# The down projection of three FFNs by seven products: a two-layer hybrid decoder step on one core

## The reference

```python
def swiglu_half(x, g, w_up, w_down):
    h = rmsnorm(x, g)
    gate, up = jnp.split(h @ w_up, 2, axis=-1)
    return x + 0.5 * ((jax.nn.silu(gate) * up) @ w_down)
```

## Time and profile before

| | us |
|---|---|
| median of 3 runs | 2964.17 |
| lowest and highest | 2961.67, 2966.86 |
| the profiled execution | 2963.34 |
| its span in the profile | 2961.5 |

### The profile page before, as it was taken

One profiled execution on the slowest core, in us unless ns is written; L12 is line 12 of the kernel. 1 busy time (PEld: TensorE's weight loads), 2 busy tenths in 40 slices (PEclk: granted clock), 3 DMA queues, 4 the chain that ended last, 5 costly groups with the idle time before them and its releaser, 6 DMA issues.

```text
span 2961.5 us, 59957 instructions
## 1 busy us (share of the span) xinstructions
PE 2904.4 (98%) x23276; PEld 2823.8 (95%) x23276; DVE 1607.9 (54%) x2331; ACT 926.6 (31%) x1555; POOL 1604.1 (54%) x1466
## 2 busy tenths in 40 slices
PE   8999999999999999999999999999999999999998
PEld 8999999989989899999999999999999989999998
DVE  7463775534432567373784737745343334783745
ACT  4121233032132325252452524321302423351423
POOL 6676676545553575425455244765555545744343
PEclk9999999999999999999999999999999999999999
DMA  5786859745521344353444433797364223443532
GB/s 196 191 258 193 213 170 283 181 160 150 137 86 58 111 141 139 128 170 111 128 142 132 160 115 106 234 243 208 117 163 124 78 69 103 156 149 120 171 118 84
DMA packets 196941, 444.05 MB, mean 150 GB/s; under 512 B 13464, under 2 KB 57664, under 8 KB 195904
## 3 DMA queue, kind: packets, MB, share of 16 engines
q1 hardware_dynamic: 106944, 280.08, 29.2%
q0 software_dynamic: 40128, 125.83, 17.7%
q10 hardware_dynamic: 49664, 35.30, 3.9%
HBM read 422.64 MB, written 144.35 MB: 191 GB/s over the span
## 4 chain that ended last, share of the span: by engine, by line
PE 88%; DVE 7%; PEld 1%; ACT 1%; DMA 1%; issue 1%; POOL 0%; ACTq 0%; DVEq 0%; POOLq 0%
PE dense L681 53%; PE SA L741 14%; PE SB L741 11%; PEld dense L681 1%; PE SA L881 1%; PE SA L968 1%; PE SA L867 1%; DMA raw<-wst 1%; PE SA L952 1%; PE SA L808 1%; DVE tmp L1479 1%; DVE Hl L1484 1%; PE SB L964 1%; PE SA L955 1%; PE SA L852 0%
## 5 line engine op out<-in xcount | busy, mean ns | idle before, releaser
L551 POOL TENSOR_SCALAR Wh<-raw 128x512 fp32r<-128x512 f32 x620 | 458.0, 739 | 787.6 <-PEq L686 509.3
L553 POOL TENSOR_TENSOR Wl<-raw,Wh 128x512 fp32r<-128x512 f32 x620 | 853.4, 1376 | 51.7
L681 PE MATMUL dense<-Hh,Wh 128*128 128x272 f32 x2784 | 592.2, 294 | 22.5 <-DVE Hl L1470 10.5
L681 PE MATMUL dense<-Hh,Wl 128*128 128x272 f32 x2784 | 577.9, 289 | 0.0
L681 PE MATMUL dense<-Hl,Wh 128*128 128x272 f32 x2784 | 576.8, 289 | 0.0
L681 PEld LDWEIGHTS dense<-Hh,Wh 128*128 128x128 f32 x2784 | 438.8, 189 | 36.3 <-issue 21.9
L681 PEld LDWEIGHTS dense<-Hl,Wh 128*128 128x128 f32 x2784 | 439.9, 190 | 0.0
L681 PEld LDWEIGHTS dense<-Hh,Wl 128*128 128x128 f32 x2784 | 437.4, 190 | 0.0
L616 POOL TENSOR_TENSOR Sl<-pair,Sh 128x512 fp32r<-128x512 f32 x120 | 171.4, 1447 | 411.6 <-ACT Sh L1048 410.8
L681 PE MATMUL dense<-Ah,Wh 128*128 128x272 f32 x1408 | 292.6, 289 | 0.1
L681 PE MATMUL dense<-Al,Wh 128*128 128x272 f32 x1408 | 290.5, 287 | 0.0
(11 more groups left out here) (459 smaller groups left out, 6294.6 us busy)
## 6 DMA issues: line engine op xcount, KB each, us to landing
raw<-wst SPq DMA_DIRECT2D x276, 512.0 KB, 3.6
w_sums<-wst POOLq DMA_DIRECT2D x36, 1536.0 KB, 13.9
w_sums<-wst POOLq DMA_DIRECT2D x18, 2048.0 KB, 16.5
pair<-wst SPq DMA_DIRECT2D x120, 256.0 KB, 3.5
pair<-w_sums SPq DMA_DIRECT2D x60, 512.0 KB, 3.7
wsum<-w_sums SPq DMA_DIRECT2D x60, 512.0 KB, 3.6
w_sums<-w_sums POOLq DMA_DIRECT2D x12, 1536.0 KB, 12.3
wsum<-wst SPq DMA_DIRECT2D x60, 256.0 KB, 2.6
```

What stands on the lines that cost most here:

```text
L551: pool.tensor_scalar(Wh[:, j, cs], raw[:, j, cs], 1.0, 0.0, ALU.mult, ALU.add).then_inc(glink, 1)
L553: pool.tensor_tensor(Wl[:, j, cs], raw[:, j, cs], f32(Wh[:, j, cs]), ALU.subtract).then_inc(glink, 1)
L681: mm = pe.matmul(dps[slot][:, a, 0:HALF], w[:, ring, w0:w0 + 128], x[:, k, a * HALF:(a + 1) * HALF], start=(k == 0 and n == 0), stop=(k == ...
```

## The change

In the FFNs `f` = 1, 2, 3 the first 16 inner tiles go through the down projection by seven products too. The weights of two output tiles, eight inner tiles deep, are again 2 by 2 groups of four blocks, so four steps do what eight dense tiles did. The last six inner tiles stay dense.

For that, each pair of inner tiles (tile t and t + 4 of a block) is also needed in four mixtures of token halves. GpSimd makes them in the step after the pair is complete (`mixed_sums`, four operations of 272 columns), ScalarE makes their high part (`mixed_hi`, 1088 columns in one), GpSimd the low part (`mixed_lo_part`, 1088 columns in one). The inner tiles are therefore done in the order `HIDDEN`, and kept in high and low parts in `PH`, `PL`, `QH`, `QL`; two of the four sets lie where `raw`, `Wh` and `Wl` are, which are not used then. The first step of a down block waits before its second product for the mixtures' low parts (`mix_lo`).

An inner tile's split is moved from the end of its step to the step after (`hidden_behind`), and the step order is written out (`STEPS`): 7 up, 4 down, 8 up, 4 down, 5 up. One up step lies between a block's last inner tile and its down steps. The low part of A22 goes from VectorE to GpSimd. On GpSimd the order inside a step is: sums of a pair, lows of S2 and S1, low of the mixtures, low of A22. The sums of the down weights need 16 more transfers for each of the three FFNs: issued at mixer pieces 54 to 84 for `f` = 1 and 3, and one per step in `f` = 1 for `f` = 2. The 24 others move from pieces 1 to 45 to pieces 6 to 52. The pieces of the dense last block are loaded and split during the last three steps.

```diff
+HIDDEN = [b * FF_BLOCK + p // 2 + p % 2 * (FF_BLOCK // 2) for b in range(2) for p in range(FF_BLOCK)]
+HIDDEN += range(2 * FF_BLOCK, FF_TILES)
...
+STEPS = [("up", i) for i in range(FAST_AT[1] + 1)] + [("down", o) for o in range(DOWN_PAIRS)]
+STEPS += [("up", i) for i in range(FAST_AT[1] + 1, FAST_AT[2] + 1)]
+STEPS += [("down", DOWN_PAIRS + o) for o in range(DOWN_PAIRS)]
+STEPS += [("up", i) for i in range(FAST_AT[2] + 1, FAST)]
+LAST_DOWN = [s for s, x in enumerate(STEPS) if x[0] == "down" and x[1] % DOWN_PAIRS == DOWN_PAIRS - 1]
+LATE = (FAST_AT[1], FAST_AT[2])
+assert len(STEPS) == PAIRS
+SUM_AT = (1, FF_BLOCK, 2 * FF_BLOCK, FF_TILES)
...
-BY_DVE, BY_POOL = (A11, A12, S3, S4, A22), (S2, S1)
+BY_DVE, BY_POOL = (A11, A12, S3, S4), (S2, S1, A22)
...
 PIECE_BASE = [EXTRA + l * STREAM for l in range(DEPTH)]
 SUM_STEPS, THREE_STEPS = 6, 2
-SUMS_AT = (*range(1, 28, 3), *range(3, 28, 3), 38, 39, 41, 42, 44, 45)
+SUMS_AT = tuple(range(6, 54, 2))
+DOWN_SUMS_AT = tuple(range(54, 86, 2))
...
-                done = ONE + LOW0[f] + (i - 1) * DVE_LO
+                if what == "down" and i % DOWN_PAIRS == 0:
+                    c = i // DOWN_PAIRS
+                    sp.wait_ge(sum_down[c], 16 * SUM_STEPS * f)
+                    sp.sem_inc(pair_began, 1)
+                    sp.wait_ge(sum_down3, 16 * THREE_STEPS * (2 * (f - 1) + c + 1))
...
-                sp.wait_ge(q_lo_pool, ONE + POOL0[f] + i * POOL_LO)
+                sp.wait_ge(q_lo_pool, ONE + POOL0[f] + (s * POOL_LO - 1 if s else 0))
                 sp.dma_start(pair[:, S2:S1 + 1, :], w_sums[0:2, n, :, :].rearrange("s p c -> p s c")).then_inc(s21_in, 16)
                 low_made(A12)
                 sp.dma_start(slot(A12), wst[at, :, 512:1024]).then_inc(a12_in, 16)
                 low_made(S4)
                 sp.dma_start(wsum[:, 0:2, :], w_sums[2:4, n, :, :].rearrange("s p c -> p s c")).then_inc(s34_in, 16)
-                low_made(A22)
+                sp.wait_ge(q_lo_pool, ONE + POOL0[f] + s * POOL_LO)
...
+                def last_down(m):
+                    load(p0 + DOWN_AT[0][2] + m, d0 + 6 * FF_BLOCK + 2 * FF_LAST + m, m % 2, FF_LAST * P)
+                for s in range(1, PAIRS):
+                    load_seven(f, s)
+                    if s == PAIRS - 3:
+                        sp.wait_ge(prod_done, 7 + (PAIR0[f] + LAST_DOWN[1] + 1) * 7)
+                        sp.sem_inc(pair_began, 1)
+                        last_down(0)
+                        last_down(1)
...
+            def down_sums(f, at):
+                if at < 12:
+                    sum_step(f, 3 + at % 2, at // 2)
+                else:
+                    three_step(f, 3 + (at - 12) // 2, at % 2)
+            def mixed_sums(f, which, hp):
+                if hp:
+                    pool.wait_ge(pair_mid, (UP0[f] + 2 * hp - 1) * 3 + 3)
+                else:
+                    pool.wait_ge(slot_free[1], ONE + TILE_BASE[f // 2] // 2 + ((0, FFN2_T0)[which] // 2 + 2))
+                pool.sem_inc(split_began, 1)
+                n = HID_PAIRS * (f - 1) + hp
+                if n:
+                    pool.wait_ge(mix_lo, n)
+                    pool.sem_inc(split_began, 1)
+                h0, h1 = slice(0, HALF), slice(HALF, TOK)
+                E, O, T = tmp[:, 0, :], tmp[:, 1, :], mixed[which]
+                pool.tensor_tensor(T[:, 0, :], E[:, h0], E[:, h1], ALU.subtract).then_inc(mix_sum, 1)
+                pool.tensor_tensor(T[:, 1, :], E[:, h1], O[:, h1], ALU.subtract).then_inc(mix_sum, 1)
+                pool.wait_ge(mix_sum, 4 * n + 1)
+                pool.tensor_tensor(T[:, 3, :], T[:, 0, :], O[:, h1], ALU.add).then_inc(mix_sum, 1)
+                pool.wait_ge(mix_sum, 4 * n + 3)
+                pool.tensor_tensor(T[:, 2, :], T[:, 3, :], O[:, h0], ALU.subtract).then_inc(mix_sum, 1)
+            def mixed_lo_part(f, which, hp):
+                pool.wait_ge(mix_hi, HID_PAIRS * (f - 1) + hp + 1)
+                pool.tensor_tensor(mixed_lo(which, hp % 4), mixed[which], f32(QH[hp % 4][:, :, :]),
+                                   ALU.subtract).then_inc(mix_lo, 1)
...
-                    for m in range(1, KT):
-                        one(p0 + DOWN_AT[0][b] + m, nf * P)
+                for s, (what, i) in enumerate(STEPS):
+                    mixes = what == "up" and i % 2 == 0 and i <= LATE[1]
+                    if mixes:
+                        mixed_sums(f, which, i // 2)
+                    if s + 1 < PAIRS:
+                        lows(f, s + 1, (S2, S1))
+                    if mixes:
+                        mixed_lo_part(f, which, i // 2)
+                    if s + 1 < PAIRS:
+                        lows(f, s + 1, (A22,))
+                    if f == 1 and s < 16:
+                        down_sums(2, s)
+                    if s >= PAIRS - 3:
+                        one(p0 + DOWN_AT[0][2] + s - (PAIRS - 3), FF_LAST * P)
+                for m in range(3, KT):
...
+                def fast(i, part, sums_made=None):
...
+                                pe.wait_ge(mix_lo, sums_made)
                         if copied:
                             pe.wait_ge(prod_copy, n * 2 + copied)
                         if read:
                             pe.wait_ge(prod_read, n * 5 + read)
...
+                    elif b == 0:
+                        for s, (what, i) in enumerate(STEPS):
+                            if what == "up":
+                                fast(s, normed)
+                                continue
+                            c = i // DOWN_PAIRS
+                            if i % DOWN_PAIRS == 0:
+                                pe.wait_ge(ffn_lo, f * FF_TILES + FF_BLOCK * (c + 1))
+                                pe.sem_inc(step_began, 1)
+                            fast(s, hidden_part, HID_PAIRS * (f - 1) + (c + 1) * HID_PAIRS // 2)
+                    if b < 2 and not alternate:
...
+                def hidden_hi(h):
+                    j = h % 2
+                    if h >= 2 * FF_BLOCK:
+                        ins = act.activation(Ah[:, h - 2 * FF_BLOCK, :], tmp[:, j, :], ACT.Copy)
+                    elif j == 0:
+                        ins = act.activation(PH[h % FF_BLOCK // 2][:, 0, :], tmp[:, 0, 0:HALF], ACT.Copy)
+                    else:
+                        ins = act.activation(PH[h % FF_BLOCK // 2][:, 1:3, :], halves(tmp[:, 1, :]), ACT.Copy)
+                    ins.then_inc(ffn_hi, 1)
...
+                def mixed_hi(hp):
+                    act.wait_ge(mix_sum, 4 * (HID_PAIRS * (f - 1) + hp) + 4)
+                    act.activation(QH[hp % 4][:, :, :], mixed[which], ACT.Copy).then_inc(mix_hi, 1)
+                def up_products(s, i):
...
+                    ahead(s, A11, S2)
+                    hidden_behind(s)
                     act.wait_ge(ffn_lo, t - 1)
+                    if i < 2 * FF_BLOCK:
+                        act.wait_ge(mix_sum, 4 * (HID_PAIRS * (f - 1) + i // 2) + (2, 4)[j])
+                    if i - 1 in LATE:
+                        act.wait_ge(down_x, 3 * 2 * DOWN_PAIRS * (f - 1) + 3 * DOWN_PAIRS * (LATE.index(i - 1) + 1))
                     act.wait_ge(prod_done, 7 + n * 7 + 3)
                     act.activation(tmp[:, j, HALF:TOK], SB[:, 0, 0:HALF], ACT.Copy).then_inc(prod_copy, 1)
-                    if ahead:
-                        for q in (S1, A12, S3, S4):
-                            high(f, a + i + 1, q)
+                    ahead(s, S1, A12)
+                    if j == 0 and i <= LATE[1]:
+                        mixed_hi(i // 2)
+                    ahead(s, S3, S4)
                     act.wait_ge(prod_read, n * 5 + 7)
-                    act.wait_ge(pair_mid, n * 3 + 2)
+                    act.wait_ge(pair_mid, u * 3 + 2)
                     act.activation(tmp[:, 4 + j, :], tmp[:, 4 + j, :], ACT.Silu).then_inc(silu_done, 1)
-                    if ahead:
-                        high(f, a + i + 1, A22)
-                    act.wait_ge(pair_mid, n * 3 + 3)
-                    act.activation(Ah[:, hidden_at(i, a, b), :], tmp[:, j:j + 1, :], ACT.Copy).then_inc(ffn_hi, 1)
+                    ahead(s, A22)
...
+                def down_products(s, d):
+                    n, e = PAIR0[f] + s, 2 * DOWN_PAIRS * (f - 1) + d
+                    act.wait_ge(prod_read, n * 5 + 3)
+                    act.wait_ge(prod_done, 7 + n * 7 + 1)
+                    act.activation(tmp[:, 3, 0:HALF], SA[:, 0, 0:HALF], ACT.Copy).then_inc(prod_copy, 1)
+                    ahead(s, A11, S2)
+                    if e:
+                        act.wait_ge(down_x, 3 * e - 2)
+                    act.wait_ge(prod_done, 7 + n * 7 + 3)
+                    act.activation(tmp[:, 5, HALF:TOK], SB[:, 0, 0:HALF], ACT.Copy).then_inc(prod_copy, 1)
+                    ahead(s, S1, A12, S3, S4, A22)
...
+                def up_products(s, i):
+                    n, u = PAIR0[f] + s, UP0[f] + i
+                    t = L * (2 * FF_TILES) + (which * FF_TILES + 2) + i
```

(51 more changed lines are left out.)

276 lines of the change are left out of this document (176 added, 100 removed).

## The result

The changed kernel takes 3004.3 us (median of 4 runs, 3000.5 to 3016.7) against 2965.2: ratio 1.0147, interval 1.0133 to 1.0161. It is slower by 1.5%; the forecast was 2948, with a range of 2926 to 2970, and "slower" had a chance of 0.15. The profiled execution took 3000.45 us.

What follows compares the result with a forecast made beforehand. TensorE, busy 98% of the span, was taken to bound the kernel. 2963.3 - 36.2 (matmuls removed) + 17.4 (stalls in six blocks) + 3 (transfers in the first FFN) = 2947.5; beside the median 2948 us, range 2926 to 2970.

Steps and rivals of the forecast that it cites:

- The 288 matmuls: Six down blocks: 48 fewer TensorE matmuls each, at 0.1256 us, all on the path; 36.2 us saved.
- ScalarE's copy: Up steps: one more ScalarE copy of 1088 columns per two steps, 1.3 us taken, no cost by itself.
- GpSimd's long subtraction: Even up steps: one GpSimd subtraction of 1088 columns per pair, 2.55 us taken, bounds 2.5 to 3.8.
- turns by whole instructions: VectorE and GpSimd at the port: each holds the other for its own instruction's time less about 0.14 us.
- the second product of the first down step: Entry of a down block: TensorE waits 1.35 us for the last pair's long subtraction; 8.1 us over six.
- the list: Expected TensorE waits: first down step's second product (1 to 2 us, six times); first read or copy in odd steps.
- the walk: Up steps followed instruction by instruction with port turns: 1.55 us for three pairs, 2.9 a block, 17.4 for six.
- The odd step works most of the lag off: Odd up step after a pair: lag mostly recovered, next pair's sums 0.6 late, costing 0.65 us.
- the lag adds up: Rival in up steps: later pairs start 2 us late, 7.7 us per block, 2977 us; chance 0.28 including partly so.
- The ledger: Port time in two up steps: 20.5 us of VectorE and GpSimd turns in 21.1, so the order decides.
- The first of the FFNs: First of the three FFNs: GpSimd's 16 added transfer issues delay the sums; 3 us taken, between 0 and 7.
- The mixers: Moved and added sum transfers in the mixers: zero taken, plus and minus 3 us.

Runs made afterwards that it cites:

- e6: The changed kernel with the low part of A22 back on VectorE, last in its step; 2990.4 us.
- e1: The changed kernel with VectorE's read of the sixth product queued ahead of its low part of S3 in an up step; 3001.1 us.
- e7: The changed kernel with a mixer's 24 old sums back at pieces 1 to 45, the 16 new ones unmoved; 3000.0 us.
- e8: The changed kernel with the 16 transfers of f = 1 issued in the first mixer instead, at pieces 55 to 85; 3031.6 us.
- e10: The changed kernel with TensorE's wait for mix_lo at the second product's fourth inner tile, and sum transfers moved and spread; 3004.2 us.
- e5: The changed kernel with GpSimd's long subtraction one step later, in the odd step, for pairs not last in a block; 3006.2 us.
- e2: The changed kernel with the long subtraction of 1088 columns split into four of 272; 3000.7 us.
- e4: The changed kernel with both edits of e1 and e2: read ahead of S3's low, long subtraction in four pieces; 3005.0 us.
- e3: The changed kernel with the long subtraction on VectorE, between its low of S4 and the gate, not on GpSimd; 2986.7 us.
- e9: The changed kernel with the long subtraction on VectorE in the odd step, except a block's last pair, kept in its own step; 2990.1 us.
- e12: The changed kernel with long subtraction (one step later) and low of A22 on VectorE, TensorE's mix_lo wait at the fourth inner tile; 2976.6 us.
- e13: e12 with a block's last long subtraction ahead of product 6, sums at pieces 1 to 45 and 48 to 78, three-steps every fourth; 2964.7 us.
- e16: e13 with all sums issued at the changed kernel's pieces; 2970.6 us.
- e11: The changed kernel with a pair's sums and long subtraction on VectorE, and TensorE's mix_lo wait at the fourth inner tile; 2977.8 us.
- e15: e13 with the sums of a pair on VectorE too, GpSimd keeping the lows of S2 and S1; 2960.2 us.
- e17: e15 with a pair's sums ahead of the low of A11 and of the inner tile's low part; 2960.0 us.

## Why the prediction was wrong

**What held.** The 288 matmuls at 0.1256 us; a step still 10.55 us where nothing waits; ScalarE's copy (1.1 us, 1.3 taken); GpSimd's long subtraction (2.67 to 2.99 us, 2.55 taken from the earlier trace rows); turns by whole instructions (a low of VectorE 3.02 us behind one of 2.75); the PSUM reads never stretched (0.42 to 0.44, all 300 in the up steps). And most of the places: TensorE stopped at the second product of the first down step, at the first read and at the copy in odd steps, as listed. The largest wait, for VectorE's read of product 6, was not on the list.

**The step that failed** is this one of the walk: "The odd step works most of the lag off; the next pair starts its sums 0.6 late and costs 0.65." The first pair of a block came out nearly as walked. In the step shown above (begun at 2633.46) the long subtraction ran from 9.1 to 11.9 us instead of 10.5 to 12.9, the gate product ended at 13.2 as in the walk, and TensorE lost 0.5 us, not 0.25 (0.8 in the other block of that FFN). But the odd step behind it worked nothing off. GpSimd's lows lay across it too. Last of all its low of A22, which the change had moved from VectorE, held VectorE's last value, and the next pair's sums wait for that value (that step began at 2655.03):

```profile
2657.72 1.31 POOL L715 TENSOR_TENSOR Sl<-wsum,Sh 128x512 fp32r<-128x512 f32 x1 [4.93 <-ACT Sh L1190]
2659.89 1.31 POOL L699 TENSOR_TENSOR mixedM<-tmp 128x272 f32<-128x272 f32 x1 [0.86 <-DVE tmp L1857]
```
```profile
2658.26 1.35 DVE L1857 TENSOR_TENSOR tmp<-tmp 128x544 f32<-128x544 f32 x1
```

The sums began 4.9 us into their step, 2.1 later than the 2.8 of the walk and not 0.6; in all twelve such pairs of the last two FFNs it is 4.7 to 5.2. Their long subtraction then ended some 14.6 us after the start of their step, with the gate product behind it, and such a pair cost 3.2 us, not 0.65. The first down step cost 2.65 (1.9 of it the wait for the long subtraction), not 1.35. e6 supports this reading: with the low of A22 back on VectorE two steps take 23.1 us, 1.2 less.

That is the condition of the rival "the lag adds up": "If the second and third pair of a block start 2 us late, not 0.6". It was the right mechanism, had 0.28, and was itself too cheap: 2 us a pair and 7.7 a block, where a pair cost 3.2 and 66 us over six blocks are 11 a block.

A second thing in the walk was wrong: whose turn it is. The walk served VectorE's low of S3 ahead of the long subtraction. In the trace GpSimd's next instruction follows its last at once, and the low comes behind it, with the read of product 6 and the gate product behind that low. In e1 the read goes ahead; in the same pair the long one ended at 2671.16 and the gate product at 2672.07, and TensorE waited 1.46 for the copy. The four kernels that change the order alone give 0.3 to 0.9 us of the 3.2 of a pair, so this is the smaller part.

**The ledger.** The prediction said: "20.5 us of turns in 21.1. It fits only just, so the order decides." The two steps took 24.3. The sum that the later forecasts used adds all of VectorE's work in two up steps (14.7 us) to GpSimd's at the port (13.4): 28.1 us. It counts eight reads of PSUM (0.43 each) where there are ten, so every sum in this table should be 0.9 higher; the differences stay. In the last FFN, which has no transfers of sums in it, and in TensorE's starts in the last two FFNs:

| kernel | sum, us | two steps, us | first down step, us | f = 3, us |
|---|---|---|---|---|
| after, e7, e8, e10 | 28.1 | 24.3 | 13.2 to 14.2 | 368.8 to 369.9 |
| e5, e1 | 28.1 | 24.0, 23.7 | 12.7 to 14.2 | 368.0, 368.4 |
| e2, e4 | 28.1 | 23.5, 23.4 | 15.5 to 16.9 | 370.4, 370.7 |
| e6 | 26.9 | 23.1 | 14.6 | 366.0 |
| e3, e9 | 26.7 | 23.1, 23.2 | 13.2 to 14.7 | 364.4, 364.2 |
| e12, e13, e16 | 25.7 | 22.5 to 22.8 | 12.1 to 14.9 | 357.5 to 359.9 |
| e11 | 25.4 | 22.3 to 22.4 | 11.9 | 357.7 |
| e15, e17 | 24.3 | 22.3, 22.4 | 11.9, 13.2 | 357.8, 358.3 |

Without any waits two steps would be 21.1 and f = 3 361.5 - 12.06 = 349.4. The first row is one and the same FFN but for e10's wait, and e13 and e16 are the same FFN with 359.9 and 357.5: a difference of 2.4 us in f = 3 says nothing by itself. Part of it is the clock. These 17 kernels have 68 first down steps in their last two FFNs: the 25 that took 14.1 us and more all have a granted clock of 0.50 for 3.4 or 6.8 us in them, and the other 43, at most 13.4 us, have none. In the changed kernel such a stretch cost 1.0 us (14.2 against 13.2). Eight kernels at one sum lie within 2.7 us there. 1.2 us less of work take 1.2 from two steps, 2.4 less take 1.7, and below 25.7 little more is to be had. So amount came before order, and the two steps show it more clearly than the stage, where the first down step blurs it. Over all three FFNs it is less clear: e1 and e5, which change the order alone, won 11 and 8 us, e6 12. Most of e1's and e5's gain is in f = 1, beside the transfers.

What is not shown is why the sum works. Every one of these kernels has the same ten reads of PSUM, and only work that uses the port was moved. So the time at the port alone (each sum less the reads, 24.6 for the changed kernel) orders them just as well, and no run separates the two. That VectorE's own load is what remains at 24.3 is argued from its 103.76 of 112 us, not shown by a run.

The rule of the Trainium skill, SBUF — State Buffer, section Who interferes with whom, was no part of the failure: the rows after agree with it. It says that the two engines exclude each other, and also that the order of issue decides who waits. In the step shown the long subtraction was issued 0.27 us ahead of the low of S3, and the low waited. The walk had these two the other way round. What the rule doesn't say is how a queue carries a lag from one step into the next, and that is where the walk went wrong.

**The first of the FFNs.** 3 us were taken, with a bound of 7; e8 measured 7.1. The term was mis-sized by 4.

**The mixers.** Zero was taken, plus and minus 3: 0.5 and 6.8 in the profiled execution, up to 17 in a mixer of a variant that leaves the transfers where the change put them (e9, 735.5). The text had named the state load that "could take longer beside them", and looked at the one near the end of a mixer. The ones that grew belong to the first branch: before, the row of sums had a gap from 606 to 702 us, and the change filled it. It put nothing for a sum's issue that waits for the sum before and holds up a weight split, 4.9 us in the second mixer.

**The sum redone.** 2963.3 - 36.2 + 59.4 (19.1, 20.8 and 19.5 of waits in the three FFNs) + 7.1 (transfers in f = 1) + 7.3 (mixers) = 3000.9; the profiled execution took 3000.45. These terms are read off the stages, so that they add up is bookkeeping and no test. In f = 2 about 1 us of the 20.8 is the clock: behind the second entry it was granted at 0.50 (1755 to 1758 us).

## What to carry to other kernels

Walk the second and the third repetition, not only the first: a lag that cost 0.5 us in the first pair (0.25 walked) cost 3.2 in every later one, since nothing in between worked it off. When two engines exclude each other at the memory and their work only just fits, don't count on an order that fits, and take work off first: here that gave twice what the best order gave in the steps with pairs. Check an order also where it ends (the first down step), and not only where it helps. A long instruction in a queue is paid by everything behind it, also by what needs no port. Before transfers are moved or added, look where the old ones left a gap, which small load or store on the path used it, and whether an issue has to wait for the transfer before it.

## What was not expected of the hardware

- A short stop of TensorE costs about 0.24 us more than its row says. In the changed kernel:

```profile
2698.51 0.29 PE L874 MATMUL SA<-Mh,Sl 128*128 128x272 f32 x1
2699.08 0.36 PE L874 MATMUL SA<-ThH,Sh 128*128 128x272 f32 x1 [0.28 <-DVE tmp L1831]
2699.28 0.29 PE L874 MATMUL SA<-TlH,Sh 128*128 128x272 f32 x1
```

  From the first start to the third are 0.77 us, two matmuls of the pace are 0.25: 0.52 lost where 0.28 is listed, because idle time is counted from an end 0.29 after the start (the next would have started at 0.126), and the one after the stop takes 0.20. In the last FFN the listed waits come to 15.2 us in 25 stops (1.3 us in one stop before), and the stage lost 19.5.
- GpSimd's 1088 columns took 2.67 to 2.99 us in all 24 cases, so it was hardly ever held there, while VectorE's subtractions of 512 columns went up to 3.5 us from 0.68.
- The first branch's state loads of 512 KB, issued in the gap of the sums, landed in 3.8 to 5.1 us. In the changed kernel seven of the eight took 7.8 to 14.8, with a sum of 1.5 to 1.8 MB in flight, and in e1 a store took 14.7 in place of 3.4.
